# A hybrid RWKV-7, Mamba-2 and short-convolution layer on one core: head sums over the whole array, low-rank logits in fp32r, two steps of a triangular solve moved

## The reference, cut to what matters

```python
p = rmsnorm(x, norm_w) @ w_in
decay_logit = w0 + tanh(dw) @ w2          # rank 64: dw is 256 x 64, w2 is 64 x 1024
a = sigmoid(a0 + da @ a2)                 # rank 64 as well
kk = k * k_k
kh = kk / max(sqrt(sum_over_head(kk * kk)), 1e-12)      # key norms
# delta-rule scan over the tokens, with kh, decay, a -> y
var = mean_over_head((y - mean)**2)                     # the variance
yn = (y - mean) * rsqrt(var + eps) * ln_w + ln_b
```

## Time and profile before

| what | value |
|---|---|
| time, median of 3 runs | 1116.33 us (1116.11 to 1116.51) |
| the profiled execution: its own time, its span | 1117.01 us, 1115.3 us |
| granted TensorE clock, mean | 0.996 |
| PE busy, PEld busy | 1100.5 us (99%), 918.8 us (82%) |
| DVE, ACT, POOL busy | 807.8 us (72%), 610.7 us (55%), 42.5 us (4%) |
| chain that ended last | PE 98%, DVE 1%, ACT 1% |
| one visit | about 68 us, eight visits from about 101 us on |

### The profile page before, as it was taken

The page is one execution under the profiler, slowest core; times in us unless marked ns, Lnnn a source line. Parts: engine busy times, 40 slices in busy tenths (PEclk is TensorE's granted clock), DMA queues, the critical chain, the costliest instruction groups (busy, mean ns, idle before and its releaser), DMA issues.

```text
span 1115.3 us, 22920 instructions
## 1 busy us (share of the span) xinstructions
PE 1100.5 (99%) x8006; PEld 918.8 (82%) x8006; DVE 807.8 (72%) x1257; ACT 610.7 (55%) x934; POOL 42.5 (4%) x68
## 2 busy tenths in 40 slices
PE   7999999999999999999999999999999999999997
PEld 5888888888888888888888888888888888888885
DVE  6888889798897988889888858445555555556564
ACT  6666575665756657576475645445344544435443
POOL 2000000000000000000000120000000000000000
PEclk8999999999999999999999999999999999999999
DMA  7766656556475655656556565666666576667663
GB/s 200 206 162 181 171 141 171 157 160 167 129 189 148 180 152 141 183 144 176 143 164 176 153 189 156 222 207 189 191 191 196 158 226 200 195 179 270 212 192 109
DMA packets 254556, 197.24 MB, mean 177 GB/s; under 512 B 23111, under 2 KB 206640, under 8 KB 254128
## 3 DMA queue, kind: packets, MB, share of 16 engines
q1 hardware_dynamic: 251748, 195.81, 60.6%
q10 hardware_dynamic: 2764, 0.85, 0.3%
HBM read 193.71 MB, written 2.11 MB: 176 GB/s over the span
## 4 chain that ended last, share of the span: by engine, by line
PE 98%; DVE 1%; ACT 1%; ACTq 0%; issue 0%
PE ps L1372 31%; PE ps L1375 15%; PE ps L1473 12%; PE ps L1475 12%; PE ps L1474 12%; PE ps L1761 3%; PE ps L1762 3%; PE ps L1760 3%; PE ps L1507 1%; PE ps L1685 1%; PE ps L1546 0%; PE ps L1402 0%; PE ps L1645 0%; PE ps L1709 0%; PE ps L1554 0%; PE ps L1582 0%
## 5 line engine op out<-in xcount | busy, mean ns | idle before, releaser
L853 DVE TENSOR_TENSOR wlo<-raw,whi 128x1024 fp32r<-128x1024 f32 x352 | 434.3, 1247 | 218.4 <-ACT whi L455 216.6
L1372 PE MATMUL ps<-hx,whi 128*128 128x512 f32 x1424 | 516.2, 405 | 1.4 <-DVE hx L884 1.3
L455 ACT ACTIVATE whi<-raw 128x1024 fp32r<-128x1024 f32 (+1 forms) x356 | 370.3, 1051 | 252.8 <-PE ps L1475 182.4
L1375 PE MATMUL ps<-hx,wlo 128*128 128x256 f32 x1424 | 399.6, 281 | 0.0
L1372 PEld LDWEIGHTS ps<-hx,whi 128*128 128x128 f32 x1424 | 268.0, 188 | 69.1 <-issue 6.9
L1375 PEld LDWEIGHTS ps<-hx,wlo 128*128 128x128 f32 x1424 | 269.8, 189 | 1.1 <-DVE lots L893 0.5
L1473 PE MATMUL ps<-whi,hx 128*128 128x512 f32 x384 | 150.4, 392 | 0.0
L1475 PE MATMUL ps<-whi,hx 128*128 128x512 f32 x384 | 149.6, 390 | 0.0
L1474 PE MATMUL ps<-wlo,hx 128*128 128x512 f32 x384 | 149.5, 389 | 0.0
L1475 PEld LDWEIGHTS ps<-whi,hx 128*128 128x128 f32 x384 | 72.1, 188 | 15.0
L1473 PEld LDWEIGHTS ps<-whi,hx 128*128 128x128 f32 x384 | 72.1, 188 | 14.9 <-issue 0.2
(11 more groups left out here) (285 smaller groups left out, 1048.4 us busy)
## 6 DMA issues: line engine op xcount, KB each, us to landing
raw<-in_w_in SPq DMA_DIRECT2D x548, 256.0 KB, 3.2
raw<-in_w_branch SPq DMA_DIRECT2D x96, 256.0 KB, 3.7
raw<-in_w_out SPq DMA_DIRECT2D x64, 256.0 KB, 3.7
o<-in_x SPq DMA_DIRECT2D x4, 512.0 KB, 5.6
o<-in_x SPq DMA_DIRECT2D x2, 1024.0 KB, 8.7
acb<-acs_rows SPq DMA_DIRECT2D x7, 256.0 KB, 3.4
out_y<-lots SPq DMA_DIRECT2D x5, 256.0 KB, 2.5
lots<-in_final_norm_w SPq DMA_DIRECT2D x1, 1024.0 KB, 11.5
```

Of the source, the lines that this page charges most:

```text
L455: sc.activation(whi[:, slot, :, 0:width], raw[:, slot, :, 0:width], ACT.Copy).then_inc(hi_done, 1)
L853: tt(wlo[:, slot, :, :], raw[:, slot, :, :], whi[:, slot, :, :].bitcast(F32), ALU.subtract).then_inc(lo_done, 1)
L1372: mm(ps[:, bank, :], whi[:, slot, k, wcol], hx[:, kt].rearrange("p a t -> p (a t)"), start=first, stop=False, skip_group_check=True)
L1375: return mm(ps[:, bank, 0:T], wlo[:, slot, k, wcol], hhi[:, kt, :], start=False, stop=last, skip_group_check=True)
```

## The change

- TensorE: the key norms and the variance are one 128 x 128 fp32 matmul of 256 columns each, against the whole `head1`. The logits come first and are stacked: `lrs` holds the high part of the rank-64 activations in one half of the partitions and the low part in the other, the weight is held twice, and each logit is two 128-row fp32r matmuls (with `lorah` and `loral`). The variance goes behind the L1709/L1710 products in its slot.
- VectorE: `kk_floor` is one instruction. The steps of slots 10 and 12 stand in front of the weight subtraction of their slot instead of at the end of the slot. Two subtractions for `lrs` come once, in the preparation.
- ScalarE: one square root in place of three; one copy `lorah` for each visit (slot 13). GpSimd: one subtraction `loral` for each visit.
- SP: `load_lora` is four DMAs in place of two and stands behind chunk c+7 in place of behind chunk c+15.
- Some semaphores are merged, with no other effect.

```diff
@@ SP
             def load_lora(j):
-                sp.dma_start(lorat[0:64, 0, :], rw_w2[0, :, bass.ds(j * P, P)]).then_inc(lora_in, 16)
-                sp.dma_start(lorat[64:128, 1, :], rw_a2[0, :, bass.ds(j * P, P)]).then_inc(lora_in, 16)
+                for w, src in enumerate((rw_w2, rw_a2)):
+                    for h in range(2):
+                        sp.dma_start(lorat[side(h), w, :], src[0, :, bass.ds(j * P, P)]).then_inc(lora_in, 16)
...
                 strip(c + 4, (SC0 + j * P, SC0 + W + j * P))
+                if not last:
+                    sp.wait_ge(s["lora_mm"], j + 1)
+                    load_lora(j + 1)
                 cols = (SC0 + 2 * W + j * P, SC0 + 3 * W + j * P)
...
                     strip(c + 12, cols, quarters=range(1, 4))
-                    sp.wait_ge(s["lora_mm"], j + 1)
-                    load_lora(j + 1)
@@ GpSimd, behind scx in each visit, and once at the start
+            def lora_split_lo(j):
+                pool.wait_ge(s["lora_hi"], j + 1)
+                gp.tensor_tensor(loral[:], lorat[:], lorah[:].bitcast(F32), ALU.subtract).then_inc(s["lora_lo"], 1)
@@ ScalarE, slot 13 of each visit, and once at the start
+            def lora_split_hi(j):
+                act.wait_ge(lora_in, j * 64 + 64)
+                sc.activation(lorah[:], lorat[:], ACT.Copy).then_inc(s["lora_hi"], 1)
...
-                        sc.activation(nrm[:, 0:P], C[:, 0:P], ACT.Sqrt, scale=1.0 / 64, bias=eps3[:, 1:2])
-                        for e in range(2):
-                            op = sc.activation(nrm[side(e), P:T], B[side(1 - e), P:T], ACT.Sqrt, scale=1.0 / 64,
-                                               bias=eps3[side(e), 1:2])
-                        op.then_inc(s["var_rt"], 1)
+                        sc.activation(nrm, C[:, 0:T], ACT.Sqrt, scale=1.0 / 64, bias=eps3[:, 1:2]).then_inc(s["var_rt"], 1)
@@ VectorE
-            def kk_floor(j, bank):
+            def kk_floor(j):
                 dve.wait_ge(s["kk_mm"], j + 1)
-                ts(ksq[:, 0:P], B[:, 0:P], 1e-24, None, ALU.max)
-                for e in range(2):
-                    op = ts(ksq[side(e), P:T], ps[side(1 - e), bank, T:T + P], 1e-24, None, ALU.max)
-                op.then_inc(s["kk_max"], 1)
+                ts(ksq, B[:, 0:T], 1e-24, None, ALU.max).then_inc(s["kk_max"], 1)
...
                 for t in range(2 * (LAST + GATES) if last else SLOTS):
+                    if t == 10:
+                        for k in range(5, 8):
+                            solve_step(k)
+                        solve_corner(8)
+                    if t == 12:
+                        solve_corner(9)
+                        dve.wait_ge(s["sol_r"], j * 9 + 9)
+                        v.tensor_copy(sol_l, sol_t.rearrange("p s t -> p t s")).then_inc(s["sol_tr"], 1)
                     if t % 2 == 0 and t // 2 < nchunks and t not in (V_ST, V_ST + 2):
                         split_lo(base + t // 2 + AHEAD, (t // 2 + AHEAD) % RING)
@@ TensorE
-            def norm_and_logits(j, bank):
-                for h in range(2):
-                    for e in range(2):
-                        op = mm(ps[side(e ^ h), bank if h else 5, h * T:h * T + P], head1[side(e), side(e)],
-                                ksq[side(e), h * P:h * P + P], start=True, stop=True)
-                op.then_inc(s["kk_mm"], 1)
-                pe.wait_ge(lora_in, j * 32 + 32)
-                mm(A[:, 0:T], lorat[0:64, 0, :], lr[0:64, :], start=True, stop=True)
-                mm(C[:, 0:T], lorat[64:128, 1, :], lr[64:128, :], start=True, stop=True).then_inc(s["lora_mm"], 1)
+            def norm_and_logits(j):
+                pe.wait_ge(s["lora_lo"], j + 1)
+                for w, dst in enumerate((A[:, 0:T], C[:, 0:T])):
+                    mm(dst, lorah[:, w, :], lrs[:, w, :], start=True, stop=False)
+                    op = mm(dst, loral[:, w, :], lrs[:, w, :], start=False, stop=True)
+                op.then_inc(s["lora_mm"], 1)
+                mm(B[:, 0:T], head1[:], ksq, start=True, stop=True).then_inc(s["kk_mm"], 1)
```

More of the change, by code:

```diff
@@ L167, in build_program @@
         lorat = sb("lorat", [P, 2, P])
-        lr = sb("lr", [P, T])
+        lorah, loral = (sb(n, [P, 2, P], F32R) for n in ("lorah", "loral"))
+        lrs = sb("lrs", [P, 2, T], F32R)
         rowst = sb("rowst", [P, 24])
@@ L407, in main @@
                 if not last:
+                    lora_split_lo(j + 1)
                     kk_unit(j + 1)
+            lora_split_lo(0)
             pool.wait_ge(s["sc_mm"], NG)
@@ L559, in _ @@
                     act.wait_ge(s["ranks_sh"], 1)
-                    sc.activation(lr[0:64, :], lshift[0:64, :], ACT.Tanh)
-                    sc.activation(lr[64:128, :], lshift[64:128, :], ACT.Copy).then_inc(s["lr_ok"], 1)
+                    sc.activation(lshift[0:64, :], lshift[0:64, :], ACT.Tanh).then_inc(s["lr_ok"], 1)
+                    act.wait_ge(s["lr_ok"], 1)
+                    for w in range(2):
+                        op = sc.activation(lrs[side(w), w, :], lshift[side(w), :], ACT.Copy)
+                    op.then_inc(s["lr_ok"], 1)
                     act.wait_ge(s["dt_v"], 1)
                     sc.activation(dts[:, 2, :], dts[:, 1, :], ACT.Exp, scale=-1.0).then_inc(s["dt_e"], 1)
-                    sc.activation(dtc[:, 2:3], dtc[:, 1:2], ACT.Exp).then_inc(s["dt_ae"], 1)
+                    sc.activation(dtc[:, 2:3], dtc[:, 1:2], ACT.Exp).then_inc(s["dt_e"], 1)
                     act.wait_ge(s["dt_v"], 2)
@@ L643, in main @@
                         low(strip0, 1, BANKS[0], zp[:, 0, :])
+                    if t == 13 and not last:
+                        lora_split_hi(j + 1)
                     if t == 17:
@@ L919, in _ @@
                     dve.wait_ge(s["lora_mm"], 1)
-                    kk_floor(0, 6)
+                    kk_floor(0)
                     kk_recip(0)
@@ L953, in _ @@
                 if c == 24:
+                    dve.wait_ge(s["lr_ok"], 2)
+                    for w in range(2):
+                        op = tt(lrs[side(1 - w), w, :], lshift[side(w), :], lrs[side(w), w, :].bitcast(F32), ALU.subtract)
+                    op.then_inc(s["lr_lo"], 1)
                     fold_shift(0, 1, 0)
@@ L1223, in main @@
                         shift(j + 1, 0)
-                        kk_floor(j + 1, 7)
+                        kk_floor(j + 1)
                     if t == 34:
@@ L1695, in main @@
                     if t == V_VAR:
-                        if last:
-                            pe.wait_ge(s["ysq_ok"], j + 1)
-                        for h in range(2):
-                            for e in range(2):
-                                op = mm(ps[side(e ^ h), 6 - h, h * P:h * P + P], head1[side(e), side(e)],
-                                        ysq[side(e), h * P:h * P + P], start=True, stop=True)
-                        op.then_inc(s["var_mm"], 1)
                         pe.wait_ge(s["xst_ok"], j + 1)
@@ L1712, in main @@
                         op.then_inc(s["yb_mm"], 1)
+                        if last:
+                            pe.wait_ge(s["ysq_ok"], j + 1)
+                        mm(C[:, 0:T], head1[:], ysq, start=True, stop=True).then_inc(s["var_mm"], 1)
             with pe.Fori(0, CT - 1) as j:
```

41 lines of the change are left out of this document (17 added, 24 removed).

## The result

| what | before | after |
|---|---|---|
| median of the comparison | 1115.98 us (1115.01 to 1116.51, 6 runs) | 1123.76 us (1123.46 to 1125.31, 6 runs) |
| ratio | | 1.0072, 95% interval 1.0062 to 1.0082 |
| profiled execution: own time, span | 1117.01, 1115.3 us | 1125.31, 1123.6 us |
| granted clock, mean | 0.996 | 0.995 |

The changed kernel is slower by 7.8 us. The forecast was 1127.2, the range 1122 to 1132. The clock is the same; the profile shows the time lost in waits.

A forecast was written before the change was run, and what follows sets the result against it. TensorE's stream was taken as the bound (PE busy 99%). Waits of 7 x 1.7 = 11.9 less TensorE's saving of 1.0 gave +10.9 on the profiled 1117.01, so 1127.9, given as 1127.2 against the median; range 1122 to 1132.

The forecast's parts named there:

- `ad` late: SP's queue: four earlier lorat DMAs delay the solve's input by 1.78, so VectorE starts the steps 0.5 late.
- rival 1: The solve's input lands in time; waits of 1.2 a visit at slots 18 and 19; +7.5, 1123.8; chance 0.20.
- Slot 16: TensorE waits 0.4 for VectorE's subtraction of chunk c+8, done at 193.90 but wanted at 193.53.
- `tb` held: SP's queue: the solve's result, ready sooner, stands behind chunk c+12's later load and is sent 1.89 later.
- Rival 3: Chunk c+12's load does not wait for c+8's subtraction; only slot 16's 0.4 a visit remains; +1.9, 1118.3; chance 0.05.
- Rival 2: tb's packets stand behind weights up to 0.94 more; 2.65 a visit, +17.5, 1133.9; chance 0.12.
- Slot 18: TensorE waits 0.86 in front of the slot's last matmul, for VectorE's L1119 result, ready at 198.83, wanted at 197.97.
- Slot 19: TensorE waits 0.40 for VectorE's L1129 result, done at 201.83 but wanted at 201.43.
- A visit's waits: TensorE's three waits, with some 0.05 for a semaphore: 1.7 us a visit, in 7 visits, 11.9.
- The small terms: At the start, two more SP DMA issues (1.3 us) and two more VectorE subtractions (about 0.8), each once, taken as nothing.
- TensorE's own saving: New section behind slot 33 saves 0.19, the variance costs 0.06 more, each 8 times; together -1.0 us.
- Rival 5: Leaving tiled matmuls saves 0.1 more at each of 16 places; -2.6, 1113.7; chance 0.05.

The follow-up runs named there:

- e3_both_back: The best version, third experiment: changed kernel with load_lora back behind chunk c+15 and the solve's steps back at their slots' ends; 1110.95 us, ratio 0.9955.
- the second experiment: Changed kernel with the triangular steps back at the end of slots 10 and 12, load_lora left early; 1115.92 us, ratio 1.0000.
- e10_tiled_variance_last: Kernel before with its four tiled variance matmuls behind the products that followed them; 1115.67 us, ratio 1.0003.
- e7_variance_only: Kernel before with only the variance changed: one whole-array matmul behind the two product groups, one square root; 1115.80 us, ratio 1.0000.
- e6_norms_only: e3_both_back with the variance in its old tiled form and place and three square roots, so only norms and logits are new; 1114.44 us, ratio 0.9989.
- e9_norms_before_logits: e3_both_back with the key norms' whole-array matmul ahead of the stacked logits instead of behind them; median 1113.27 us, ratio 0.9977.

## Why the prediction was right, and where it was not

**The sign and the mechanism** were right: both steps by which something comes late are where the prediction put them, and each has an experiment that takes it away alone.

- **`ad` late.** Forecast start 180.31, measured 183.27 - 2.95 = 180.32. The first step of the solve: forecast 184.28, measured 187.28 - 2.95 = 184.33. This also rules out rival 1: VectorE does wait for the input. That the measured 1123.76 lies by rival 1's 1123.8 is chance; two errors make it up.
- **Slot 16.** Forecast 0.40, measured 0.44. What I had left out are the longer pairs at slots 14 and 16, 0.10 each: 0.24 with the rounding of the slots.
- **`tb` held.** Forecast 1.89 late, measured 198.01 - 2.95 - 193.33 = 1.73. L1119 forecast at 198.40, measured 198.13. Rival 3 is out. Rival 2, longer landing behind weight packets, is out too: L1119 starts 201.08 - 199.40 = 1.68 after the end of the last `tb` issue, against 1.65 before.
- **Slot 18.** Forecast 0.86, measured 0.65 in visit 1 (0.56 to 0.79 in all). **Slot 19.** Forecast 0.40, measured 0.34. The first is smaller since L1119 came 0.27 earlier than I had it, and the matmul was due 0.16 later (201.08 - 2.95 = 198.13 against 197.97). Against that work the 0.14 from the end of L1119 to the matmul and the 0.08 that a stopped stream loses, both of which I had not in the sum: 0.86 - 0.27 - 0.16 + 0.14 + 0.08 = 0.65.
- **A visit's waits** sum to 0.44 + 0.24 + 0.65 + 0.34, about 1.7, as forecast; that it is so exact is luck, since terms too large and terms left out cancel. Visit 0 has more: one `lorat` issue took about 1.5 there in place of 0.65, `ad` was waited for 1.74, and slot 13 stopped for 1.17. All seven make 13.4, the forecast was 11.9.
- **The small terms.** What I had costed at nothing in the preparation does not show: visit 0 begins at 101.26 against 101.06, and traces of kernels with the same preparation differ by more.
- **The whole.** The forecast was 10.9 us slower, the measurement 7.8. Waits that were 1.5 too small and a saving that was 4.3 too small work against each other, so the time came out nearer than the terms.

SP and VectorE at the `lorat` issues of visit 0:

```profile
109.32 1.17 SPq L268 DMA_DIRECT2D lorat<-in_rw_w  x2
110.58 2.19 SPq L268 DMA_DIRECT2D lorat<-in_rw_a  x2
```

```profile
118.08 0.15 DVE L1052 TENSOR_TENSOR lots<-lots 32x2 f32<-32x2 f32 x1 [1.74 <-DMA lots<-ad]
```

**The term that was mis-sized** is TensorE's own saving: "Together 8 x (-0.19 + 0.06) = -1.0 us". It measured -5.3 over seven visits, and the run of the best version confirms it with 5.0. PE behind slot 33 of visit 0 after, against the earlier trace rows:

```profile
162.71 0.28 PE L1393 MATMUL ps<-hx,wlo 128*128 128x256 f32 x1
162.82 0.28 PE L1415 MATMUL ps<-lrs,lorah 128*128 128x256 f32 x1
162.94 0.28 PE L1416 MATMUL ps<-lrs,loral 128*128 128x256 f32 x1
163.06 0.28 PE L1415 MATMUL ps<-lrs,lorah 128*128 128x256 f32 x1
163.18 0.28 PE L1416 MATMUL ps<-lrs,loral 128*128 128x256 f32 x1
163.30 0.59 PE L1418 MATMUL ps<-lots,head 128*128 128x256 f32 x2
163.54 0.59 PE L1390 MATMUL ps<-hx,whi 128*128 128x512 f32 x1
...
164.08 0.39 PE L1390 MATMUL ps<-hx,whi 128*128 128x512 f32 x1
```

From 162.71 to 163.54 it is 0.83, not 1.03: the fp32 matmul lets the next start 0.24 behind it, where I had taken 0.43 from the earlier trace rows, with another fp32 matmul behind it. The pair behind then takes 0.54 in place of the 0.45 of before. Together 1.37 against 1.22 + 0.45 = 1.67, so 0.30 saved (0.34 by the lengths of slots 33 and 34, which also hold some of the faster pace). At the variance's place the two slots grow from 2.67 + 1.51 to 2.64 + 1.58, by 0.04. That is 0.30 a visit net, against my 0.13. Another 0.03 to 0.12 lies in slot 4. In visit 0 alone that slot is 0.43 longer than before, in the changed kernel and in the best version: TensorE comes to it earlier, and its last matmul then waits for VectorE (`L1392 <- DVE lots L909` in the list above). The rest, 0.3 to 0.7 a visit, is the pace of the plain slots. Rival 5 had the direction of this, and its size was too small: -2.6 where -5 was measured. It could not decide, as `tb` was 1.73 later.

On tiles, the Trainium skill, TensorEngine Tiling (Array Packing), Theoretical Speedup, would have made the whole-array form the slower one; in the runs, the version with the whole-array sums and the stacked logits is the faster by 5.0 us. (The +2.4 us that I had worked out from that rule counted 0.06 twice at each place: 16 x 0.21 less 8 x 0.25 for the logits is +1.4.) On the early load, the Trainium skill, DMA: Bandwidth & Descriptors, Rules for kernel authors, has the advice to issue early and wait late. Here the issue itself was the cost: the early one is 5.0 us slower in the second experiment than the late one in the third.

## What to carry to other kernels

In a queue that is worked in order, look at what each entry waits for, and at what stands behind it: the solve's result, ready early, stood behind a load that waited for work which had been moved behind the solve. When VectorE's work is swapped, ask which queue entry waits for the piece that fell back. A change whose parts have opposite signs (here -5, +5.6 and +7) should be timed part by part: the useful part alone, `e3_both_back`, beats both kernels at 1110.95 us.

## What the runs showed of the hardware that was not expected

**Two paces of the same stream at the same clock.** Four pairs of large matmuls take 1.39 us or 1.41 to 1.42, at a granted clock of 0.994 to 0.996 in all these runs. A stretch of slots mostly keeps its pace until something else comes between. What stood at the variance's place ahead of slot 30 and in the section behind slot 33, and the pace that followed, in the one trace of each kernel ("tiled" is the 64 x 64 form, ahead of the products in 128 x 64 tiles or, where it says last, behind them):

| kernel | variance | slots 30 to 32 | last matmul of the section | slots 35 to 38 |
|---|---|---|---|---|
| before | tiled | 1.41 | fp32, 64 rows | 1.41 |
| `e10_tiled_variance_last` | tiled, last | 1.41 | fp32, 64 rows | 1.41 |
| `e7_variance_only` | whole array, last | 1.39 | fp32, 64 rows | 1.41 |
| `e6_norms_only` | tiled | 1.41 | fp32, whole array | 1.39 |
| `e9_norms_before_logits` | whole array, last | 1.39 | fp32r, whole array | 1.41 |
| best, after | whole array, last | 1.39 | fp32, whole array | 1.39 |

At these two places the fast pace follows where a whole-array fp32 matmul is the last one ahead of the stream, at the price of a longer first pair. `e9_norms_before_logits` shows that order alone switches it. It is no rule for the whole visit, and why it is so is open. No run changed the stream itself. A stop can be followed by either pace (the one in slot 39 of `e6_norms_only` by 1.41, those in slots 14 to 16 of the changed kernel by 1.39 in some visits and 1.42 in others). The same instructions also come at both paces in one execution: in the kernel before, slots 5 to 17 take 1.41 in visits 2, 4 and 6 and 1.39 in the others, which makes these visits 68.4 long instead of 68.05, and slots 1 to 3 take 1.39 in visits 1, 3 and 5 and 1.41 in the others, with only large matmuls since slot 34. Which visits have slow slots 5 to 17 also differs between traces: 4 and 6 in `e7_variance_only`, 2 in `e6_norms_only`, none in `e10_tiled_variance_last`.

**A wait costs TensorE more than its idle time says.** The bracket of 0.28 cost 0.44 and 0.10 in the next pair. Where TensorE waited for VectorE behind slot 18, the matmul started 0.14 to 0.15 after the end of VectorE's instruction, with its weight load stopped by the same wait, so an instruction that ends less than that ahead of the matmul's due time is already late.
